# Clearing a stage's semaphores by ranges, and the semaphores of stages that end together in one block

## What is computed

```
def swiglu(h, w_up, w_down):
    gate, up = jnp.split(h @ w_up, 2, axis=-1)
    return (jax.nn.silu(gate) * up) @ w_down

def run_trunk(x, c, pos0, P, past, page_table):
    c_act = jax.nn.silu(c)
    for layer in range(DEPTH):
        mod = c_act @ P['w_mod'][layer] + P['b_mod'][layer]
        sh1, sc1, g1, sh2, sc2, g2 = [m[:, None, :] for m in jnp.split(mod, 6, axis=-1)]
        h = rms_norm(x, P['norm_mix'][layer]) * (1.0 + sc1) + sh1
        y = mix_ab(h, ...) if layer % 2 == 0 else mix_nsa(h, ...)
        x = x + g1 * y
        h = rms_norm(x, P['norm_ffn'][layer]) * (1.0 + sc2) + sh2
        x = x + g2 * swiglu(h, P['w_up'][layer], P['w_down'][layer])
```

## Time and profile before

| | before |
|---|---|
| median of 3 runs | 2416.56 us |
| lowest, highest | 2413.52, 2420.88 us |
| profiled execution, its own time | 2417.96 us |
| its span, first to last instruction | 2416.3 us |
| TensorE busy | 2071.7 us, 86% |
| VectorE busy | 1360.7 us, 56% |
| ScalarE busy | 787.1 us, 33% |
| GpSimd busy | 272.1 us, 11% |
| mean granted TensorE clock | 0.913 |

### The profile page before, as it was taken

How to read it: one execution, slowest core, us unless ns; L and a number is a source line. 1 busy time by engine, 2 the same in 40 slices (tenths; PEclk the granted TensorE clock), 3 DMA queues, 4 the chain that set the end, 5 groups by cost and what they waited for, 6 DMA issues and landing times. The chain is left out here.

```text
span 2416.3 us, 48234 instructions
## 1 busy us (share of the span) xinstructions
PE 2071.7 (86%) x18117; PEld 1865.8 (77%) x18117; DVE 1360.7 (56%) x2556; ACT 787.1 (33%) x1407; POOL 272.1 (11%) x436
## 2 busy tenths in 40 slices
PE   4987797688999897997879996989987776999898
PEld 2873574386999896895569886988974475999898
DVE  3435431257888643446365657777743357888732
ACT  2211331114555301212246654544431214545300
POOL 0101333200000000000022212212223200000000
PEclk8996898798999998998789997999988898999999
DMA  8416789735333221224420004333449612333231
GB/s 345 131 45 254 246 294 365 283 111 159 97 98 106 96 87 40 62 83 181 174 91 1 2 1 145 112 105 113 118 140 339 237 62 70 105 100 93 90 96 62
DMA packets 237726, 322.60 MB, mean 134 GB/s; under 512 B 18235, under 2 KB 194440, under 8 KB 230063
## 3 DMA queue, kind: packets, MB, share of 16 engines
q1 hardware_dynamic: 215767, 240.34, 30.6%
q0 software_dynamic: 21728, 79.19, 9.5%
HBM read 311.56 MB, written 16.42 MB: 136 GB/s over the span
## 5 line engine op out<-in xcount | busy, mean ns | idle before, releaser
L2557 PE MATMUL ps<-CHi,W1H 128*128 128x256 f32 x768 | 221.7, 289 | 38.0 <-DVE CLo L2660 38.0
L2558 PE MATMUL ps<-CLo,W1H 128*128 128x256 f32 x768 | 219.7, 286 | 0.0
L2559 PE MATMUL ps<-CHi,W1L 128*128 128x256 f32 x768 | 219.5, 286 | 0.0
L897 PE MATMUL ps<-XHup,WLup 128*128 128x272 f32 x640 | 185.1, 289 | 0.0
L897 PE MATMUL ps<-XHup,WHup 128*128 128x272 f32 x640 | 183.8, 287 | 1.3 <-DVE G L1046 1.3
L897 PE MATMUL ps<-XLup,WHup 128*128 128x272 f32 x640 | 184.5, 288 | 0.0
L2557 PEld LDWEIGHTS ps<-CHi,W1H 128*128 128x128 f32 x768 | 150.0, 195 | 40.0 <-DVE CLo L2660 29.6
L443 PE MATMUL ps<-XHdn,WHdn 128*128 128x272 f32 x704 | 148.2, 292 | 14.7 <-DMA TOK<-in_cache_fox_v 6.5
L2078 DVE TENSOR_REDUCE NM<-ps 128x1 f32<-128x128 f32 (+1 forms) x224 | 89.6, 403 | 116.4 <-PE ps L1957 80.4
L2558 PEld LDWEIGHTS ps<-CLo,W1H 128*128 128x128 f32 x768 | 150.1, 195 | 0.0
L2559 PEld LDWEIGHTS ps<-CHi,W1L 128*128 128x128 f32 x768 | 149.9, 195 | 0.0
(11 more groups left out here) (562 smaller groups left out, 5339.6 us busy)
## 6 DMA issues: line engine op xcount, KB each, us to landing
H<-in_w_up SPq DMA_DIRECT2D x72, 512.0 KB, 4.9
Wearly<-in_w_mod SPq DMA_DIRECT2D x24, 1024.0 KB, 11.2
RAWdn<-in_w_down SPq DMA_DIRECT2D x14, 1408.0 KB, 6.3
RAWin<-in_nsa_w_in SPq DMA_DIRECT2D x20, 512.0 KB, 3.7
RINGf<-in_cache_fox_k SPq DMA_DIRECT2D x34, 256.0 KB, 5.6
Wmod<-in_w_mod SPq DMA_DIRECT2D x8, 1024.0 KB, 17.0
Wlate<-in_w_mod SPq DMA_DIRECT2D x8, 1024.0 KB, 8.3
G<-in_w_up SPq DMA_DIRECT2D x16, 512.0 KB, 5.4
```

Source lines behind the costliest of these rows:

```text
L897: last = self.nc.tensor.matmul(self.ps[:, bank + b, 0:HALF], wt[:, w, k, :], x[:, k, :], start=start and k == 0 and n == 0, stop=k == 3 an ...
L2557: nc.tensor.matmul(out, WH[:, sig, k, w], hi, start=(k == 0 and m == 0), stop=False, skip_group_check=True)
L2558: nc.tensor.matmul(out, WH[:, sig, k, w], lo, start=False, stop=False, skip_group_check=True)
L2559: last = nc.tensor.matmul(out, WL[:, sig, k, w], hi, start=False, stop=(k == KU - 1), skip_group_check=True)
```

## The change

At the end of a stage its tensors are given back, but its semaphores are only put on a list (`self.ended`). The list is worked off by `flush`, which runs when the next stage begins, and once more after `finish`: one Block clears the semaphores of all stages on the list. In it, `dma_reset` spans all their numbers, and `sem_clear` is called once for each run of consecutive numbers, with a range.

```diff
@@ -90,37 +90,47 @@
         self.top = ExitStack()
         self.stages = 0
+        self.ended = []
 
     @contextmanager
     def stage(self):
 
         nc = self.nc
+        self.flush()
         self.stages += 1
         number = self.stages
+        semaphores, made = ExitStack(), []
         with ExitStack() as held:
-            made = []
-
             def sb(name, shape, dt=F32):
                 return held.enter_context(nc.sbuf_tensor(f"{name}_{number}", shape, dt))
 
             def sem(name):
-                made.append(held.enter_context(nc.semaphore(f"{name}_{number}")))
+                made.append(semaphores.enter_context(nc.semaphore(f"{name}_{number}")))
                 return made[-1]
 
             yield sb, sem
-            if made:
-                self.clear(made)
+        self.ended.append((semaphores, made))
+
+    def flush(self):
+
+        made = [s for _, m in self.ended for s in m]
+        if made:
+            self.clear(made)
+        while self.ended:
+            self.ended.pop()[0].close()
 
     def clear(self, semaphores, drain=True):
 
         with self.nc.Block(no_gpsimd_drain=not drain) as block:
             @block.gpsimd
             def _(pool):
+                numbers = sorted(s.num for s in semaphores)
                 if drain:
-                    pool.dma_reset(range(min(s.num for s in semaphores), max(s.num for s in semaphores) + 1))
-                for s in semaphores:
-                    pool.sem_clear(s)
+                    pool.dma_reset(range(numbers[0], numbers[-1] + 1))
+                for a in numbers:
+                    if a - 1 not in numbers:
+                        pool.sem_clear(range(a, next(n + 1 for n in numbers if n >= a and n + 1 not in numbers)))
```

## The result

| | before | after |
|---|---|---|
| median of 4 runs | 2416.62 us | 2391.76 us |
| lowest, highest | 2413.52, 2420.88 us | 2387.85, 2394.53 us |
| profiled execution, its own time | 2417.96 us | 2387.85 us |
| its span | 2416.3 us | 2386.2 us |
| TensorE busy | 2071.7 us | 2072.1 us |

The changed kernel is 1.05% faster: ratio 0.9895, 95% interval 0.9874 to 0.9916, which is 20 to 30 us. 2388.8 us was predicted.

The account below looks back on a forecast made before the run. TensorE is busy 86% of the span; the change can touch only idle time, where clears are serial for the whole core. Terms -24.7 - 2.7 - 1.1 + 0.7 = -27.8 us from 2416.56 give 2388.8 us, range 2384 to 2395 (2380 to 2398 with two rivals).

Parts of the forecast that it names:

- Serial time of the whole core: Clearing Blocks: no engine works during clears, so the number of clear instructions, about 0.064 us each, sets their time.
- Clears removed: Clearing Blocks: 440 clears become 54, so 386 fall away at 0.064 us each, 24.7 us less.
- Blocks joined: Clearing Blocks: 29 become 21, each of the 8 saving 0.34 us beyond its clears, 2.7 us less.
- Pauses: Within lists of 47 and 53 clears and a one-clear Block at 952.7 us: three pauses gone, 1.1 us less.
- The new instructions: Range clears: each number priced at 1.7 ns, taken from the reset, 0.7 us added for 386 numbers.
- The sum: All terms over the whole kernel: 27.8 us less.
- What follows a Block: Loads behind barriers move forward with the work; only the first Block's 1.7 us might become a wait for weights.
- rival 1: Stages waiting for loads: transfers catch part of the gain; a quarter lost, 7 us, gives 2396 us; chance 0.10.
- The clock: TensorE's pauses at stage ends: shorter ones priced at nothing, with a possible gain of 1.8 us at some Blocks.
- Rival 2: TensorE's shortened pauses: five of 21 keep the clock, 9 us less in all, 2380 us; chance 0.08.
- rival 3: Range clears: each semaphore still takes a whole step, leaving -3.8 us, 2412.8 us, no measurable change; chance 0.04.
- rival 4: Work Blocks' entry branches: instruction fetches exposed, two in turn at 21 Blocks give back 45 us, 2433.8 us; chance 0.03.

Follow-up runs that it names:

- after_again: The changed kernel once more, no edit, on the same chip as its parts: 2389.31 us, ratio to before 0.9901.
- e4_lazy: The changed kernel, but clearing only when no free semaphore is left and after the last stage (4 Blocks, 10 clears): 2379.44 us, ratio to before 0.9852.
- e3_twice: The kernel before with each semaphore cleared twice (29 Blocks, 880 clears): 2446.49 us, ratio to before 1.0122.
- e7_ten: The changed kernel with its list of range clears issued ten times over (21 Blocks, 540 clears): 2442.28 us, ratio to before 1.0097.
- e1_ranges: The kernel before with range clears alone, Blocks not joined (29 Blocks, 52 clears): 2390.06 us, ratio to before 0.9908.
- e2_join: The changed kernel with one clear for each semaphore, so Blocks joined alone (21 Blocks, 440 clears): 2414.45 us, ratio to before 0.9984.
- e6_blocks: The changed kernel with two more one-clear Blocks behind each clearing Block (63 Blocks, 96 clears): 2402.01 us, ratio to before 0.9922.
- e5_five: The kernel before with each Block's single clears dealt out to all five engines (29 Blocks, 440 clears): 2393.72 us, ratio to before 0.9901.

## Why the prediction was right

**Serial time of the whole core.** Right, and this is what the prediction stood on. Over nine kernels (ten traces) whose clearing Blocks take from 4.8 to 68.1 us, the span less the Blocks stays between 2368.0 and 2376.7 us. The spread of runs of one kernel is as large: after and after_again alone ran from 2384.91 to 2397.99 us. If a tenth of the Blocks' time were absorbed, the column would fall by 6 us from e4_lazy to e3_twice and to e7_ten, which have 60 us more in their Blocks. It rises by 3.5 us to the one and falls by 4.7 us to the other. The single profiled executions exclude absorption much above a tenth. The medians are steadier: less the Blocks' sum they are 2374.6 us for e4_lazy, 2376.3 for after_again, 2378.6 and 2380.1 for the two series of before, 2377.3 for e7_ten and 2378.4 for e3_twice. A straight line through all ten medians, of before in both series and of the eight kernels measured beside it, gives 1.06 us of time for 1 us of Blocks, give or take 0.05. By that none of it is absorbed. Why the slope comes out a little above 1 is not shown.

**Clears removed, 24.7 us.** e1_ranges, which does this part alone, took 24.7 us off the Blocks, but with the cost of the ranges inside and the end of some pauses too. Those two go against each other, so this confirms the term to about 1 us and no closer.

**Blocks joined, 2.7 us.** e2_join took 2.7 us off the Blocks and 0.8 us from between them, 3.5 us in all. The 0.4 us of the prediction ran from the end of the first Block's barrier, so it already held one step of 0.06 us between Blocks, and 2.7 is to be held against the 3.5. The rest is the one longer step, 0.3 us more than the others, which "nothing else lies between" left out, and pauses, which came to 1.8 us in before and to 1.3 us in e2_join. What is left for the frames is 2.8 us.

**Pauses, 1.1 us.** In after none of the three is left. Before had more of them than I counted: the barriers that close the Blocks at 1800 and 2002 us take 0.3 us longer than the others, so all pauses together are 1.8 us. What makes a pause is not shown; neither the length of a list nor the Block alone foretells one (e2_join's list of 54 has one, its list of 44 none).

**The new instructions, 0.7 us.** Mis-sized. I took 1.7 ns a number from the reset; the clear takes 5.4, so the 386 numbers cost 2.1 us. It is the one term that missed by a factor, and the resemblance of two instructions that both take a range was no ground for a price.

**The sum.** In the two traces the clears with their ranges, pauses left out, fell by 22.7 us where the terms of 24.7 and 0.7 say 24.0; the pauses gave 1.8 us, not 1.1; and the joined Blocks with what lay between them 2.9, not 2.7. That is 27.4 us. It came as close to 27.8 as it did because a dear range and overlooked pauses went against each other, and that part is luck.

**What follows a Block.** Kept in the sum, rightly. Over the whole trace the waits of TensorE, VectorE and ScalarE that a transfer ended are 120.8 us before and 119.5 us after. From the end of the first Block, the one with full DMA, to the start of the second it is 116.8 us before and 115.8 us after. The wait for cache pages of the earlier trace rows, now 1428 to 1774 us:

```profile
DVE S L2650 <- DMA KS<-in_cache_nsa_vc: 16.0, 2, 8.7
```

16.0 instead of 16.2 us. One place does show rival 1. Behind the Block at 1166.3 us TensorE waits for a weight that it had found loaded before (the row of after, then of before, from TensorE's timelines):

```profile
1167.66 1.93 PE L303 MATMUL ps<-H,CV 128*32 128x512 f32 x8 [1.77 <-DMA H<-in_w_mod]
```

```profile
1192.50 1.94 PE L293 MATMUL ps<-H,CV 128*32 128x512 f32 x8 [1.09 <-PEq L117]
```

It starts 1.00 us behind GpSimd's last record of the Block, not 0.14 us. That gives 0.9 us back there, and in after_again the same wait is not there. So transfers caught a part in this trace, under 1 us of 27.

**The clock.** Priced at nothing, and TensorE's busy time says the same, 2072.1 against 2071.7 us. The windows on the FoX stage's end, to be laid beside the earlier trace rows; first the pause, then the work behind it:

```profile
core 0: us, PE busy (x) PEld busy (x) DVE busy (x) ACT busy (x) POOL busy (x), PEclk, DMA share, GB/s
461.20:466.20 5.00, 0.00 (x0) 0.00 (x0) 3.22 (x6) 3.19 (x6) 0.00 (x0) 0.72 0.38 120
466.30:470.20 3.90, 3.90 (x17) 3.90 (x18) 3.90 (x7) 1.19 (x3) 0.00 (x0) 0.50 0.32 111
470.40:474.00 3.60, 3.60 (x31) 3.60 (x30) 1.84 (x3) 0.00 (x0) 0.00 (x0) 1.00 0.01 2
```

The pause is 5.0 instead of 8.7 us, and the matmuls behind it still start at 0.50, 1.2 GHz, now for 3.9 us instead of 3.5. In e4_lazy the same pause is 4.0 us:

```profile
463.30:467.30 4.00, 0.00 (x0) 0.00 (x0) 3.22 (x6) 3.19 (x6) 0.00 (x0) 0.78 0.46 156
467.40:471.50 4.10, 4.10 (x18) 4.10 (x19) 4.10 (x8) 1.19 (x3) 0.00 (x0) 0.50 0.30 98
```

Still 0.50 behind it, for 4.1 us. Here the shorter pause kept no clock; if anything it left a little more slow work behind it. Rival 2 falls at the place of the largest saving, and the unchanged busy time leaves it nothing elsewhere.

**A range that costs by its length, rival 3.** True in kind and 12 times too small to matter: 5.4 ns a number, not 64.

**The next Block's program, rival 4.** The prediction's case for the last stage was weaker than it says: ahead of that Block of one clear stood one with 14 clears, 2404.1 to 2405.3 us, so there was a stretch of clears before it. In after the first matmul there still follows its release at once, behind a list of three. TensorE's timeline and GpSimd's records of L125 there, as the earlier trace rows:

```profile
2375.35 0.88 PE L809 MATMUL ps<-CN,X 128*128 128x128 f32 x3 [2.73 <-PEq L125]
```

```profile
L125 POOLq EVENT_SEMAPHORE  x2: 17/17/17, 2375.1 to 2375.2; - x2
```

That, the 42 Blocks of e6_blocks at 0.35 us, and e4_lazy, which leaves the sequencers no pause at all at most stage ends and is the fastest, leave nothing for it. The rule of the Trainium skill, "Runtime: NRT & Kernel Launch", section "Instruction fetch mechanics", on taken branches out of the fetched window has no case here that shows it; whether these branches leave the window isn't in the trace. The Trainium skill, "VectorE: DVE Perf Modes", section "The DRAIN you can't avoid", gives the drains of the program's frame as about 12 ns; it doesn't speak of a Block's. Counted as the prediction counted them, one behind the other, they would have made the joined Blocks worth 0.5 us; the Blocks measured 2.7. In the trace the five drains of a Block are on five engines and overlap, and GpSimd's records of reset, clear and barrier are what fills the Block's 0.33 us.

**The size of the measured gain.** 24.9 us by the medians of four runs each against 27.8 predicted and 27.4 in the Blocks. The interval of the ratio, 20 to 30 us, holds all three. No step of the prediction can be blamed for the 3 us, and none has to be.

## What to carry to other kernels

Time in barriers and semaphore instructions stands in no busy share; count those records and take the step between their starts, not their durations (0.064 us against 38 ns here). What one engine does between two barriers over all engines was worth its full length here: clear semaphores by ranges, and better, only when their numbers run out, which here was four times instead of 29. A price for an instruction in a form that the trace doesn't show needs bounds from both sides; a neighbour with the same kind of operand gave a third of the true rate.

## What the runs showed of the hardware

- A clear on GpSimd takes about 32 + 5.4 n ns for n semaphores (46 at 3, 69 at 8, 110 at 14, 180 at 27, 286 at 47). One semaphore takes 44 ns in e6_blocks and at the least in after, but 37 or 38 ns in most records of before and e2_join; why is not shown.
- Clears of one semaphore each, back to back, step at 0.06 us on GpSimd and SyncE, 0.07 on ScalarE, 0.08 on VectorE and 0.12 on TensorE, and run side by side on different engines (e5_five).
- A Block with one clear, no reset, entered and left through a barrier over five engines is 0.33 us in most cases and 0.35 us on average (e6_blocks).
